# Turning tiles through DRAM: one write in 4 KB rows and four gathering reads, in place of four writes and one read

## What is computed

```python
for i in range(DEPTH):                       # DEPTH = 4
    hn = rmsnorm(x, norm_g[i])
    kind, j = i % N_MIXERS, i // N_MIXERS
    if kind == 0:
        y = diff_attention(hn, da_w_in[j], da_w_out[j], ...)
    elif kind == 1:
        y = sliding_window_attention(hn, sw_w_in[j], sw_w_out[j], ...)
    else:
        y = mlstm(hn, ml_w_in[j], ml_b_gates[j], ml_w_out[j], ml_norm_g[j])
    x = x + y
return rmsnorm(x, final_g)
```

## Time and profile before

| | us |
|---|---|
| median of 3 runs (1711.56 to 1712.52) | 1711.88 |
| profiled execution, its own time | 1712.57 |
| its span | 1710.8 |
| TensorE busy | 1699.6 (99%) |
| VectorE busy | 1188.9 (69%) |
| ScalarE busy | 911.4 (53%) |

### The profile page before, as it was taken

How to read it: one execution, slowest core, us unless ns; L and a number is a source line. 1 busy time by engine, 2 the same in 40 slices (tenths; PEclk the granted TensorE clock), 3 DMA queues, 4 the chain that set the end, 5 groups by cost and what they waited for, 6 DMA issues and landing times.

```text
span 1710.8 us, 24445 instructions
## 1 busy us (share of the span) xinstructions
PE 1699.6 (99%) x7890; PEld 1417.7 (83%) x7890; DVE 1188.9 (69%) x1909; ACT 911.4 (53%) x1400; POOL 38.9 (2%) x99
## 2 busy tenths in 40 slices
PE   9999999999999999999999999999999999999998
PEld 7888888888888888888888888888888888888887
DVE  7767677775769888865656465656676676777756
ACT  7454555554656666655544545454554555455543
POOL 1000000000000000000000000000000000000000
PEclk9999999999999999999999999999999999999999
DMA  8768676766875555478998699966877686767673
GB/s 286 244 194 262 201 245 215 233 216 220 264 216 161 160 159 153 154 234 194 190 166 271 177 201 182 265 182 216 260 227 237 195 265 200 247 214 232 223 237 126
DMA packets 230035, 364.53 MB, mean 213 GB/s; under 512 B 14950, under 2 KB 80044, under 8 KB 229836
## 3 DMA queue, kind: packets, MB, share of 16 engines
q1 hardware_dynamic: 229536, 362.94, 73.5%
q0 software_dynamic: 48, 0.13, 0.1%
q10 hardware_dynamic: 380, 0.56, 0.1%
HBM read 335.79 MB, written 27.79 MB: 213 GB/s over the span
## 4 chain that ended last, share of the span: by engine, by line
PE 95%; DMA 2%; issue 1%; SPq 1%; DVE 1%; ACT 0%; DVEq 0%; POOLq 0%; POOL 0%; ACTq 0%
PE acc L1136 29%; PE acc L1137 29%; PE acc L1138 29%; PE tp L1102 1%; PE tp L1137 1%; PE tp L1136 1%; PE tp L1138 1%; DMA raw<-in_ml_w_in_dram 1%; PE sc L1137 1%; PE sc L1136 1%; PE sc L1138 1%; DMA xres<-in_x_dram 0%; DMA qs<-q_turning 0%; DMA q_turning<-scr 0%; PE sc L1162 0%
## 5 line engine op out<-in xcount | busy, mean ns | idle before, releaser
L2015 DVE TENSOR_TENSOR w_lo<-raw,w_hi 128x1024 fp32r<-128x1024 f32 x583 | 703.2, 1220 | 401.4 <-ACT w_hi L1074 399.0
L1074 ACT ACTIVATE w_hi<-raw 128x1024 fp32r<-128x1024 f32 x583 | 610.2, 1056 | 454.9 <-PE acc L1138 401.6
L1136 PE MATMUL acc<-w_hi,xt_hi 128*128 128x512 f32 x1824 | 715.3, 392 | 1.7 <-DVE w_lo L2015 1.0
L1138 PE MATMUL acc<-w_hi,xt_lo 128*128 128x512 f32 x1824 | 711.0, 390 | 0.0
L1137 PE MATMUL acc<-w_lo,xt_hi 128*128 128x512 f32 x1824 | 710.4, 389 | 0.0
L1138 PEld LDWEIGHTS acc<-w_hi,xt_lo 128*128 128x128 f32 x1824 | 342.4, 188 | 72.3
L1136 PEld LDWEIGHTS acc<-w_hi,xt_hi 128*128 128x128 f32 x1824 | 342.6, 188 | 70.3 <-DVE w_lo L2015 1.6
L1137 PEld LDWEIGHTS acc<-w_lo,xt_hi 128*128 128x128 f32 x1824 | 342.6, 188 | 67.3
L1136 PE MATMUL acc<-w_hi,ot_hi 128*128 128x512 f32 (+1 forms) x456 | 176.6, 387 | 0.0
L1138 PE MATMUL acc<-w_hi,ot_lo 128*128 128x512 f32 (+1 forms) x456 | 175.8, 386 | 0.0
L1137 PE MATMUL acc<-w_lo,ot_hi 128*128 128x512 f32 (+1 forms) x456 | 175.8, 385 | 0.0
(11 more groups left out here) (306 smaller groups left out, 1226.5 us busy)
## 6 DMA issues: line engine op xcount, KB each, us to landing
raw<-in_da_w_in_dram SPq DMA_DIRECT2D x255, 512.0 KB, 4.4
raw<-in_ml_w_in_dram SPq DMA_DIRECT2D x96, 512.0 KB, 5.7
raw<-in_sw_w_in_dram SPq DMA_DIRECT2D x72, 512.0 KB, 3.7
raw<-in_da_w_out_dram SPq DMA_DIRECT2D x64, 512.0 KB, 4.0
raw<-in_sw_w_out_dram SPq DMA_DIRECT2D x32, 512.0 KB, 3.7
raw<-in_ml_w_in_dram SPq DMA_DIRECT2D x64, 256.0 KB, 7.3
raw<-in_ml_w_out_dram SPq DMA_DIRECT2D x32, 512.0 KB, 3.9
qs<-q_turning SPq DMA_DIRECT2D x12, 512.0 KB, 6.9
```

Of the source, the lines that this page charges most:

```text
L1074: act.activation(w_hi[:, q:q + 2, :], raw[:, 2 * p:2 * p + 2, :], ACT.Copy).then_inc(hi_ready, 1)
L1136: pe.matmul(out_ap, k_hi, m_hi, start=start, stop=False)
L1138: return pe.matmul(out_ap, k_lo, m_hi, start=False, stop=stop)
L2015: dve.tensor_tensor(w_lo[:, two, :], raw[:, two, :], w_hi[:, q:q + 2, :].bitcast(F32), ALU.subtract).then_inc(lo_ready, 1)
```

## The change

In `write`, one DMA copies the whole block buffer, 128 partitions, each a row of 4 KB (3 KB for p), to the scratch tensor, which now holds it as it is. In `read`, four DMAs follow; the one for j gathers for the landing partitions 32j to 32j+31 the four blocks of its row, in runs of 512 bytes (768 for p). The scratch views `q_rows`, `k_rows`, `o_rows`, `x_rows` and `p_rows` are gone. `written` steps by 16 and `moved` by 64 in `COUNTS` and in every wait. Places, order, buffers and all compute instructions stay.

```diff
-    "q_written": ((0, 0, 0), (0, 64, 0), (0, 0, 0), (0, 64, 0)),
-    "q_moved":   ((0, 0, 0), (0, 16, 0), (0, 0, 0), (0, 16, 0)),
+    "q_written": ((0, 0, 0), (0, 16, 0), (0, 0, 0), (0, 16, 0)),
+    "q_moved":   ((0, 0, 0), (0, 64, 0), (0, 0, 0), (0, 64, 0)),
...
-            def write(rows, blocks, turned, value, written):
+            def write(scratch, blocks, turned, value, written):
 
                 sp.wait_ge(sig[turned], value)
-                for i in range(4):
-                    dst = rows[:, :, i, :] if rows is p_rows else rows[:, :, :, i, :]
-                    sp.dma_start(dst, blocks[32 * i:32 * i + 32]).then_inc(sig[written], 16)
-
-            def read(landing, rows, written, value, moved):
+                sp.dma_start(scratch.rearrange("p (t j r) -> p t j r", t=T, j=4) if scratch is not p_dram else
+                             scratch.rearrange("p (j r) -> p j r", j=4), blocks).then_inc(sig[written], 16)
+
+            def read(landing, scratch, written, value, moved):
 
                 sp.wait_ge(sig[written], value)
-                sp.dma_start(landing, rows).then_inc(sig[moved], 16)
+                halves = T if scratch is not p_dram else 1
+                rows = scratch.rearrange("(i n) (t j r) -> n t j i r", i=4, t=halves, j=4)
+                for j in range(4):
+                    dst = landing[32 * j:32 * j + 32].rearrange("n (t i r) -> n t i r", t=halves, i=4)
+                    sp.dma_start(dst, rows[:, :, j]).then_inc(sig[moved], 16)
...
-                    act.wait_ge(sig["q_moved"], in_iter(l, "q_moved", i, 16))
+                    act.wait_ge(sig["q_moved"], in_iter(l, "q_moved", i, 64))
```

More of the change, by code:

```diff
@@ L95 @@
     "q_turned":  ((0, 0, 0), (0, 1, 0), (0, 0, 0), (0, 1, 0)),
-    "q_written": ((0, 0, 0), (0, 64, 0), (0, 0, 0), (0, 64, 0)),
-    "q_moved":   ((0, 0, 0), (0, 16, 0), (0, 0, 0), (0, 16, 0)),
+    "q_written": ((0, 0, 0), (0, 16, 0), (0, 0, 0), (0, 16, 0)),
+    "q_moved":   ((0, 0, 0), (0, 64, 0), (0, 0, 0), (0, 64, 0)),
     "q_lo":      ((0, 0, 0), (0, 1, 0), (0, 0, 0), (0, 2, 0)),
     "p_turned":  ((0, 0, 0), (0, 1, 0), (0, 0, 0), (0, 0, 0)),
-    "p_written": ((0, 0, 0), (0, 64, 0), (0, 0, 0), (0, 0, 0)),
-    "p_moved":   ((0, 0, 0), (0, 16, 0), (0, 0, 0), (0, 0, 0)),
+    "p_written": ((0, 0, 0), (0, 16, 0), (0, 0, 0), (0, 0, 0)),
+    "p_moved":   ((0, 0, 0), (0, 64, 0), (0, 0, 0), (0, 0, 0)),
     "k_turned":  ((0, 0, 0), (0, 1, 0), (0, 0, 0), (0, 0, 0)),
-    "k_written": ((0, 0, 0), (0, 64, 0), (0, 0, 0), (0, 0, 0)),
-    "k_moved":   ((0, 0, 0), (0, 16, 0), (0, 0, 0), (0, 0, 0)),
+    "k_written": ((0, 0, 0), (0, 16, 0), (0, 0, 0), (0, 0, 0)),
+    "k_moved":   ((0, 0, 0), (0, 64, 0), (0, 0, 0), (0, 0, 0)),
     "k_lo":      ((0, 0, 0), (0, 1, 0), (0, 0, 0), (0, 0, 0)),
@@ L110 @@
     "x_turned":  ((0, 0, 0), (0, 0, 4), (0, 0, 3), (0, 0, 4)),
[6 rows of a table removed]
[6 rows of a table added]
     "x_lo":      ((0, 0, 0), (0, 0, 4), (0, 0, 3), (0, 0, 4)),
     "o_turned":  ((0, 0, 0), (0, 1, 0), (0, 0, 0), (0, 1, 0)),
-    "o_written": ((0, 0, 0), (0, 64, 0), (0, 0, 0), (0, 64, 0)),
-    "o_moved":   ((0, 0, 0), (0, 16, 0), (0, 0, 0), (0, 16, 0)),
+    "o_written": ((0, 0, 0), (0, 16, 0), (0, 0, 0), (0, 16, 0)),
+    "o_moved":   ((0, 0, 0), (0, 64, 0), (0, 0, 0), (0, 64, 0)),
     "ot_lo":     ((0, 0, 0), (0, 2, 0), (0, 0, 0), (0, 2, 0)),
@@ L579, in move_q @@
                 if (i := w.due(when["q_write"])) is not None:
-                    write(q_rows, qk_blocks[w.kind], "q_turned", in_iter(l, "q_turned", i, 1), "q_written")
+                    write(q_dram, qk_blocks[w.kind], "q_turned", in_iter(l, "q_turned", i, 1), "q_written")
                 if (i := w.due(when["q_read"])) is not None:
-                    read(flat(qs), q_dram, "q_written", in_iter(l, "q_written", i, 64), "q_moved")
+                    read(flat(qs), q_dram, "q_written", in_iter(l, "q_written", i, 16), "q_moved")
             def move_k(w, l):
                 if (i := w.due(DA["k_write"])) is not None:
-                    write(k_rows, qk_blocks["da"], "k_turned", in_iter(l, "k_turned", i, 1), "k_written")
+                    write(k_dram, qk_blocks["da"], "k_turned", in_iter(l, "k_turned", i, 1), "k_written")
                 if (i := w.due(DA["k_read"])) is not None:
-                    read(shared[:, 0:T * JW], k_dram, "k_written", in_iter(l, "k_written", i, 64), "k_moved")
+                    read(shared[:, 0:T * JW], k_dram, "k_written", in_iter(l, "k_written", i, 16), "k_moved")
             def move_p(w, l):
                 if (i := w.due(DA["p_write"])) is not None:
-                    write(p_rows, p_blocks, "p_turned", in_iter(l, "p_turned", i, 1), "p_written")
+                    write(p_dram, p_blocks, "p_turned", in_iter(l, "p_turned", i, 1), "p_written")
                 if (i := w.due(DA["p_read"])) is not None:
-                    read(p_landed, p_dram, "p_written", in_iter(l, "p_written", i, 64), "p_moved")
+                    read(p_landed, p_dram, "p_written", in_iter(l, "p_written", i, 16), "p_moved")
             def move_o(w, l):
@@ L601, in move_o @@
                 if (i := w.due(when["o_write"])) is not None:
-                    write(o_rows, o_blocks, "o_turned", in_iter(l, "o_turned", i, 1), "o_written")
+                    write(o_dram, o_blocks, "o_turned", in_iter(l, "o_turned", i, 1), "o_written")
                 if (i := w.due(when["o_read"])) is not None:
-                    read(flat(th), o_dram, "o_written", in_iter(l, "o_written", i, 64), "o_moved")
+                    read(flat(th), o_dram, "o_written", in_iter(l, "o_written", i, 16), "o_moved")
             def move_x(w):
@@ L610, in move_x @@
                     b = n % 3
-                    write(x_rows[b], x_blocks[b], "x_turned", in_out(l, "x_turned", n + 1), f"x_written_{b}")
+                    write(x_dram[b], x_blocks[b], "x_turned", in_out(l, "x_turned", n + 1), f"x_written_{b}")
                 if (ln := w.x_due("read")) is not None and not x_kept(*ln):
@@ L615, in move_x @@
                     landing = (flat(th), flat(qs), shared[:, 0:T * JW])[b]
-                    read(landing, x_dram[b], f"x_written_{b}", in_out(l, f"x_written_{b}", 64 * (n // 3 + 1)), f"x_moved_{b}")
+                    read(landing, x_dram[b], f"x_written_{b}", in_out(l, f"x_written_{b}", 16 * (n // 3 + 1)), f"x_moved_{b}")
             def moves(w):
@@ L815, in x_turned_hi @@
                 if not x_on_pe(l, n):
[L816 removed]
+                    act.wait_ge(sig[f"x_moved_{n % 3}"], in_out(l, f"x_moved_{n % 3}", 64 * (n // 3 + 1)))
                     for c in range(4):
@@ L894, in o_turned_hi @@
             def o_turned_hi(l, i):
-                act.wait_ge(sig["o_moved"], in_iter(l, "o_moved", i, 16))
+                act.wait_ge(sig["o_moved"], in_iter(l, "o_moved", i, 64))
                 for c in range(4):
@@ L1530, in o_turned_lo @@
             def o_turned_lo(l, i):
-                dve.wait_ge(sig["o_moved"], in_iter(l, "o_moved", i, 16))
+                dve.wait_ge(sig["o_moved"], in_iter(l, "o_moved", i, 64))
                 for c in range(4):
@@ L1656, in side_da @@
                 if (i := w.due(DA["q_copy"])) is not None:
-                    dve.wait_ge(sig["q_moved"], in_iter(l, "q_moved", i, 16))
+                    dve.wait_ge(sig["q_moved"], in_iter(l, "q_moved", i, 64))
                     dve.tensor_copy(in_blocks(q0[:]), q_chunks(0, 0, 4))
@@ L1666, in side_da @@
                 if (i := w.due(DA["k_copy"])) is not None:
-                    dve.wait_ge(sig["k_moved"], in_iter(l, "k_moved", i, 16))
+                    dve.wait_ge(sig["k_moved"], in_iter(l, "k_moved", i, 64))
                     dve.wait_ge(sig["qk_hi"], in_iter(l, "qk_hi", i, 2))
@@ L1702, in side_da @@
                 if (i := w.due(DA["p_copy"])) is not None:
-                    dve.wait_ge(sig["p_moved"], in_iter(l, "p_moved", i, 16))
+                    dve.wait_ge(sig["p_moved"], in_iter(l, "p_moved", i, 64))
                     dve.wait_ge(sig["p_hi"], in_iter(l, "p_hi", i, 1))
```

17 lines of the change are left out of this document (6 added, 11 removed), and 12 rows, old and new, of the table COUNTS.

## The result

The changed kernel takes 1720.17 us in the median of five runs (1716.75 to 1723.43) against 1711.88 of before: ratio 1.0043, 95% interval 1.0032 to 1.0054. It is slower, by a little but clear of the noise: 8.3 us, where the prediction took 3.4 us for the least that can be told. The forecast was no change, 1711.9; the time lies above the range, whose end was 1716.5. Its runs also lie further apart than those of before.

The account below looks back on a forecast made before the run. The prediction took TensorE to bound the kernel, busy 1699.6 of 1710.8 us, with issue and DMA work only moved. Profiled 1712.57 + 0 - 0.69 = 1711.9 us, no change; range 1710.4 to 1716.5.

Parts of the forecast that it names:

- The ceiling: TensorE's waits inside the layers: a change to transfers alone can win no more than about 1.4 us, 0.08%.
- The issuing queue: SP: issue time per tile 2.8 us before and after; 2.2 us only moves from ahead of the hand-off to behind it.
- rival 2: SP: issue of the four reads isn't hidden, each tile 1.9 us late; +5.8 us, 1717.7, slower; chance 0.08.
- the relief expected ahead of the hand-off: SP's queue before the read: emptied 2 us earlier for q, the long write landing about 3.4 us after issue.
- The q tile: Da layers, 8 times: lands 2 us earlier to 0.5 later, taken 1 earlier; slack 0.8 us, no cost at TensorE.
- The data time of the gather: DMA engines: 1.8 us per gather, bounds 1.3 and 2.9; write plus read stay 3.1 us per tile.
- The k tile: Da layers, 8 times: lateness 0, bounds -0.5 and +1.9 or +1.1; slack some 1.4 us, so cost nothing.
- The p, o and other x tiles: Tiles other than q, k and the last x: idle time behind them that no TensorE wait touches; no cost.
- The last x tile: Into the second da layer, once: slack 0.15 us, lateness taken 0; 1.1 us later would cost 0.9.
- The mLSTM layer: DMA bounds this layer, queue served in order; cost 0, from -1.4 to +3.3 us.
- rival 1: Dear short reads: DRAM gathers in 512-byte runs take 2.9 us, not 1.8; +4.2 us, 1716.1, slower; chance 0.11.
- The signs: If right: no da-layer TensorE idle, q wait below 22.1 us, issues about 0.4 and 0.6, first da layer's DMA share near 0.74.

Follow-up runs that it names:

- e_rows: Changed kernel, but each turned tile read back by one DMA in 4 KB rows, without the block swap; 1710.94 us, 0.9989 of before.
- e_spread4: Changed kernel, but four reads in 4 KB rows, each landing in every fourth partition, without the block swap; 1712.45 us, 1.0001 of before.
- e_long4: Changed kernel, but four reads in 4 KB rows, each landing in 32 neighbouring partitions, without the block swap; 1717.45 us, 1.0026 of before.
- e_after: The changed kernel measured again, unaltered, in a second series; 1717.85 us, 1.0030 of before.
- t_x: Kernel before with the change made for the 11 x tiles alone; 1717.22 us, 1.0020 of before.
- x_spread4: Kernel before, x tiles alone: one long write, four 4 KB-row reads each into every fourth partition, no block swap; 1712.84 us, 1.0001 of before.
- e_short1: Changed kernel, but one read of 128 partitions in 512-byte runs from nearby addresses, without the block swap; 1714.16 us, 1.0006 of before.

## Why the prediction was wrong

**What bounds it, and the most that can be gained: right.** The ceiling was 1.4 us. The floor, e_rows, lies 1.9 us under before, and its interval (0.3 to 3.4 us) holds the 1.4.

**The issuing queue: right, but not the relief expected of it.** The sum of issue times was put at 2.8 us on both sides. The write line of after has 0.34 to 0.63 us in the median by tensor (four mLSTM q writes up to 1.55 us), the read line 0.61 for tiles of 512 KB. That four reads stand behind the hand-off is worth about 0.1% (e_spread4 against e_rows), so rival 2 did not come true either; its price of 5.8 us would have been near the result for the wrong reason. Wrong was the relief expected ahead of the hand-off. The long write was to land 3.4 us after its issue and takes 5.0 in the median, in e_rows and e_spread4 as in after, and the four quarter writes took 5.1 from their first issue. Fewer issues did not bring the hand-off forward by as much as they saved SP.

**The q tile: issue right, landing wrong.** The four gathers of the third tile were to be issued by 238.0; SP was through with them at 238.60, 0.5 us of which is the kernel's own lateness:

```profile
236.06 2.54 SPq L569 DMA_DIRECT2D qs<-q_turning  x4
...
244.06 0.63 ACT L907 ACTIVATE q_hi<-qs 128x512 fp32r<-128x512 f32 x1 [2.63 <-DMA qs<-q_turning]
```

The kernel is 0.5 us late by then (the `w_hi` ahead of it starts at 236.49, before at 236.01), and q came 0.5 us earlier than before all the same: 1 us earlier by the kernel's own time, as forecast. But not always. In the last layer the third q tile's reads were issued from 1386.89 and ScalarE had it at 1396.60, after a wait of 5.97 us; before it was 1384.90 and 1391.71. Less the 3.2 us by which the kernel is late there (ScalarE's evacuation ahead of that wait starts at 1388.41, before at 1385.24), the tile is 1.7 us later, more than the 0.8 of slack, and TensorE waits 1.02 us at 1400.27. One tile's timeline was read as that of eight.

**The data time of the gather: the step that failed.** I took 1.8 us, from the writes of the same run length. Over e_rows, whose read I put at 1.3 and whose write is the same, the changed kernel's DMA engines work 1289.8 - 1228.9 = 61 us more in 51 tiles, 1.2 us each: 2.5 us per gather, what it costs the weight loads beside it included (2.4 in its own packets). Of this 0.4 is the short run, which the forecast had with 0.5, and most of the rest is the landing in 32 neighbouring partitions, which it had not (1.0 us per tile in e_long4). The rule was on the table. The Trainium skill, page SBUF — State Buffer, section "Door 1: The DMA port swizzle", says that partitions 0 to 31 reach 8 of the 16 ports; the estimate from it was 2.4 us. I set it aside because quarter writes out of 32 partitions ran at 294 GB/s. By that rule the runs agree for landings: spreading the 32 partitions of a DMA over the whole range takes the loss away. For transfers out of SBUF the trace of before still shows little of it (30.1 ns for a 512-byte packet, against 28.5 where a read lands in all 128 partitions). What went wrong was to carry a rate over from one direction to the other: the prediction itself said that no row decides for landings, kept 2.9 as upper bound, and then gave this case no chance or mechanism of its own, only that of dear short reads. The upper bound held.

**The k tile: slack too small for it.** The last quarter of the second k tile was issued at 165.76 and landed 6.09 us later (chain of after):

```profile
165.76 6.09 DMA shared<-k_turning
171.87 1.07 ACT kT_hi L912
173.03 1.24 DVE kT_lo L1667
```

I had expected the last quarter, issued 1.9 us after the first, to find that much less queue ahead of it, and so to land some 4.7 us after its issue. It took nearly as long as the whole read of before (6.6). In e_spread4 a k quarter lands in 3.2 us in the median, and TensorE waits for no k tile there. In after it is one wait of 0.4 us, in e_after one of 0.3.

**The x tiles: the place that was missed.** "The p, o and other x tiles have idle time behind them that no wait of TensorE touches" rested on TensorE's having no wait there. That shows that the slack is not below zero; it doesn't show its size. The last x tile, which I did examine at 0.15 us of slack, lost little: `xt_lo` came at 1267.30 against 1264.32, 3.0 us later, of which 2.75 is the kernel's own lateness, and the starts of the matmuls show 0.2 us lost there in after. The three tiles into the sliding-window layer lost 1.2 us in the profile of after and 3.3 in that of t_x. They are bunched, and the third tile's own gathers land slowly on top of a long write that is slow there also where nothing is lost (7.78 us in after, 8.5 in x_spread4).

**The mLSTM layer: the range was right.** q_lo's wait grew from 0.4 to 1.24 us, the w_lo waits shrank from 1.0 to 0.6 in sum; +0.4 was inside -1.4 to +3.3. That DMA bounds this layer did not make it the place of the loss, as rival 1 had it. Nor is the queue served strictly in order, as was assumed there: in before a weight load issued at 449.07 landed at 455.37, and the quarter write issued behind it at 450.15 had landed at 454.88.

**The signs.** Of those named for the forecast only the issue times came true: TensorE waits in the da layers, ScalarE's wait for q is 23.6 us and not under 22.1, and the DMA share of the first da layer is 0.77 and not 0.74. What I had said would show it wrong was a DMA share clearly higher, with rates under 280 GB/s where gathers run. In the stretch where the second k tile's gathers run, after has

```profile
167.00:169.00 2.00, 2.00 (x11) 1.65 (x10) 1.23 (x1) 0.34 (x2) 0.00 (x0) 1.00 1.13 222
```

222 / 1.13 = 196 GB/s. The sign named for rival 1 appeared with another cause behind it. Its price, 4.2 us, was near what the profile shows, at other places than it was worked out for.

## What to carry to other kernels

When a transfer into SBUF is cut by partitions, look at which partitions one DMA fills: 32 neighbours made these reads 1.0 us of DMA time per 512 KB dearer, while every fourth partition did not. A rate measured in one direction is no price for the other, and a rule that no row decides should get a chance of its own. Before a tile is called uncritical, work out its slack, above all where several of its kind follow one another.

## What the runs showed of the hardware

- Landing in 32 neighbouring partitions ran at 238 GB/s full-share for 4 KB rows (e_long4) and 196 with 512-byte runs (after), where spread landing ran at 379 (e_spread4), each with weight loads mixed in.
- Reads from DRAM in 512-byte runs, landing in 128 partitions, cost the DMA engines 0.4 us per tile over 4 KB rows (e_short1), no more than 512-byte quarter writes do (0.56, before against e_rows).
- Why the quarter writes out of 32 partitions suffered so little isn't settled: no run here wrote in quarters with long rows.
- That the port map is the reason for the slow landing fits all of these runs but isn't shown by itself: one other set of 32 partitions was tried, every fourth one.
- No run here does the swap and also spreads each DMA's landing over the partitions; so a kernel that does what this change wants and avoids its loss wasn't measured. With a floor of 0.1% under before it would have had little to win.
